# The first adaLN modulation as tiles of 128 channels, in a float32 trunk kernel

## The reference, cut to what matters

```python
h, hc = x, ctx                                   # 256 latent and 256 context tokens, D = 1024
silu_c, silu_cc = silu(c), silu(c_ctx)
for l in range(2):
    mod_lat = (silu_c @ ada_w[l] + ada_b[l]).reshape(b, 9, D)    # ada_w[l]: 1024 x 9216
    mod_ctx = (silu_cc @ ada_w[l] + ada_b[l]).reshape(1, 9, D)
    h = ffn_half(h, mod_lat, 0, ...)             # shift mod[0], scale mod[1], gate mod[2]
    hc = ffn_half(hc, mod_ctx, 0, ...)
    ...                                          # mixer with mod 3 to 5, second ffn_half with mod 6 to 8
return rmsnorm(h, final_norm_w)

def ffn_half(h, mod, k0, norm_w, wg, wu, wd):
    u = rmsnorm(h, norm_w) * (1 + mod[:, k0 + 1]) + mod[:, k0]
    return h + 0.5 * mod[:, k0 + 2] * ((silu(u @ wg) * (u @ wu)) @ wd)
```

## Time and profile before

| | |
|---|---|
| median of 3 runs | 1987.65 us (1984.37 to 1988.5) |
| the profiled execution, its own time | 1990.52 us |
| its span in the profile | 1988.9 us |
| mean granted TensorE clock | 0.992 |
| busy: TensorE, VectorE, ScalarE, GpSimd | 98%, 63%, 40%, 4% |

### The profile page before, as it was taken

How to read it: one execution, slowest core, us unless ns; L and a number is a source line. 1 busy time by engine, 2 the same in 40 slices (tenths; PEclk the granted TensorE clock), 3 DMA queues, 4 the chain that set the end, 5 groups by cost and what they waited for, 6 DMA issues and landing times.

```text
span 1988.9 us, 28983 instructions
## 1 busy us (share of the span) xinstructions
PE 1952.4 (98%) x10006; PEld 1654.5 (83%) x10006; DVE 1262.4 (63%) x2048; ACT 794.7 (40%) x1083; POOL 72.3 (4%) x142
## 2 busy tenths in 40 slices
PE   8999999999999999999999999999999998999998
PEld 3788888888888888888888888888888897899998
DVE  2657566676666466667576675756758687475555
ACT  2432222355654323532222354232225576456444
POOL 0000000000000000000000000000000000000000
PEclk8999999999999999999999999999999999999999
DMA  7246444433223243345445424544544333445564
GB/s 309 96 140 207 138 159 169 159 106 117 65 74 111 86 141 122 106 139 199 137 159 176 159 94 158 174 148 143 195 138 133 100 106 118 159 142 180 181 184 153
DMA packets 78664, 287.39 MB, mean 144 GB/s; under 512 B 8768, under 2 KB 10048, under 8 KB 77824
## 3 DMA queue, kind: packets, MB, share of 16 engines
q1 hardware_dynamic: 58912, 212.89, 32.4%
q0 software_dynamic: 19392, 73.34, 11.2%
q10 hardware_dynamic: 288, 0.18, 0.0%
HBM read 285.34 MB, written 1.05 MB: 144 GB/s over the span
## 4 chain that ended last, share of the span: by engine, by line
PE 93%; DMA 3%; DVE 2%; ACT 1%; issue 1%; SPq 0%; DVEq 0%; ACTq 0%
PE bank L332 26%; PE bank L334 26%; PE bank L333 26%; DMA raw<-weights 2%; PE bank L472 2%; PE bank L661 2%; PE bank L522 1%; PE bank L528 1%; PE bank L523 1%; PE bank L397 1%; PE bank L398 1%; PE bank L401 1%; ACT w_hi L684 1%; PE bank L360 1%; PE bank L605 1%
## 5 line engine op out<-in xcount | busy, mean ns | idle before, releaser
L332 PE MATMUL bank<-u_hi,w_hi 128*128 128x512 f32 (+1 forms) x1824 | 664.9, 365 | 3.5 <-DVE w_lo L950 3.4
L333 PE MATMUL bank<-u_lo,w_hi 128*128 128x512 f32 (+1 forms) x1824 | 655.2, 359 | 0.0
L334 PE MATMUL bank<-u_hi,w_lo 128*128 128x512 f32 (+1 forms) x1824 | 655.2, 359 | 0.0
L950 DVE TENSOR_TENSOR w_lo<-raw,w_hi 128x1024 fp32r<-128x1024 f32 x384 | 469.0, 1222 | 248.4 <-ACT w_hi L684 219.3
L684 ACT ACTIVATE w_hi<-raw 128x1024 fp32r<-128x1024 f32 x384 | 404.7, 1055 | 438.2 <-DMA raw<-weights 435.6
L332 PEld LDWEIGHTS bank<-u_hi,w_hi 128*128 128x128 f32 x1824 | 345.0, 189 | 55.6 <-DVE w_lo L950 4.9
L334 PEld LDWEIGHTS bank<-u_hi,w_lo 128*128 128x128 f32 x1824 | 344.7, 189 | 51.1
L333 PEld LDWEIGHTS bank<-u_lo,w_hi 128*128 128x128 f32 x1824 | 345.1, 189 | 50.6 <-issue 0.7
L332 PE MATMUL bank<-hid_hi,w_hi 128*128 128x512 f32 (+1 forms) x832 | 299.0, 359 | 1.4 <-DVE w_lo L950 1.1
L334 PE MATMUL bank<-hid_hi,w_lo 128*128 128x512 f32 (+1 forms) x832 | 298.3, 358 | 0.0
L333 PE MATMUL bank<-hid_lo,w_hi 128*128 128x512 f32 (+1 forms) x832 | 298.2, 358 | 0.0
(11 more groups left out here) (152 smaller groups left out, 1505.0 us busy)
## 6 DMA issues: line engine op xcount, KB each, us to landing
raw<-weights SPq DMA_DIRECT2D x384, 512.0 KB, 3.5
ada_raw<-adaw POOLq DMA_DIRECT2D x128, 512.0 KB, 4.2
start_w<-weights SPq DMA_DIRECT2D x8, 1024.0 KB, 12.3
box<-box POOLq DMA_DIRECT2D x4, 1024.0 KB, 8.2
h<-resid SPq DMA_DIRECT2D x1, 2048.0 KB, 19.4
silu_c<-c POOLq DMA_DIRECT2D x1, 1024.0 KB, 5.0
out<-sig_a SPq DMA_DIRECT2D x8, 128.0 KB, 2.0
poolw<-poolw POOLq DMA_DIRECT2D x2, 256.0 KB, 10.9
```

The lines of the kernel that those rows point to most:

```text
L332: pe.matmul(ps, w_hi[:, slot, k, :], hi(k), start=first, stop=False)
L333: pe.matmul(ps, w_hi[:, slot, k, :], lo(k), start=False, stop=False)
L334: mm = pe.matmul(ps, w_lo[:, slot, k, :], hi(k), start=False, stop=last)
L950: dve.tensor_tensor(view(w_lo, (j % RING) * UNIT, [1, UNIT]), raw[:, j % RING, :], view(w_hi, (j % RING) * UNIT, [1, UNIT]).bitcast(F32), ...
```

## The change

The 1024 x 2048 weights of the first shift and scale are stored as 11 column tiles and 5 row tiles of 512 KB. A column tile holds the weights of 128 output channels, with k on the partitions. It is the stationary operand, in 8 pieces of 128 x 128, and the two `silu(c)` columns move: the result is a pair of columns in a bank (`start_tile`). Scale and shift of chunks d = 0, 1, 2 (START_ROWS = 3) and the scale of d = 3 to 7 are made so; the shifts of d = 3 to 7 are made on VectorE from row tiles (`start_sum`), as the other modulation columns are.

TensorE makes the tiles of d = 0 and 1 first, those of d = 2 between the first norm's spread and the first chunk, and the one of d = k + 2 behind chunk k for k = 1 to 5. VectorE turns each into `scale_c` and `shift_c` of that chunk alone (`start_out`), and its order becomes, chunk by chunk: `start_sum`, `start_out`, `scaled`, `split_lo` (for d < 3), `low`. ScalarE's splits of the first three units and its silu of `silu_c` stand between the first chunks too. `h` is loaded in four pieces behind the first four tiles; `silu_c` moves from GpSimd's queue to SyncE's; GpSimd's other loads wait for the last `u_hi` of the first norm. The first 16 counts of `s_used` are given at the end of chunk 6. The first norm's totals go to banks 0 and 1. The copy of the masks moves behind the first part of the first FFN.

The diff, cut to its core:

```diff
+START_ROWS = 3
+START_BANK = (4, 6, 3, 4, 6, 3, 4, 6)
...
+        start_t = [sb(f"start_t{n}", [P, ND, P], F32, at_)[0] for n, at_ in enumerate(
+            [hid_hi_at + 4096 * n for n in range(8)] + [v_at, v_at + 4096, scan_at[0] + 8192])]
+        start_r, _ = sb("start_r", [P, ND - START_ROWS, D], F32, gs_at)
...
+        def total_bank(n, s):
+            return bank[s if n == 0 else 4 + 2 * s]
...
             sp.dma_start(c_cols[:], c_cols_in).then_inc(s_ccland, 16)
-            for k in range(ND):
-                sp.dma_start(start_w[k // 4][:, 2 * (k % 4):2 * (k % 4) + 2, :],
-                             weights[2 * k:2 * k + 2].rearrange("a p n -> p a n")).then_inc(s_start[k], 16)
-                if k == ND // 2 + 1:
-                    sp.dma_start(h[:], resid_in).then_inc(s_hland, 16)
-            for u in range(RING):
+            for k in range(2):
+                for j in range(2):
+                    sp.dma_start(start_t[2 * k + j][:], weights[2 * k + j]).then_inc(s_start[k], 16)
+            for k in range(ND // 2):
+                sp.dma_start(h[:, 2 * k:2 * k + 2, :], resid_in[:, 2 * k:2 * k + 2, :]).then_inc(s_hland[k], 16)
+            for j in range(2):
+                sp.dma_start(start_t[4 + j][:], weights[4 + j]).then_inc(s_start[2], 16)
+            for u in range(AHEAD):
                 sp.dma_start(raw[:, u, :], weights[START + u]).then_inc(s_raw[u], 16)
+            sp.dma_start(silu_c[:], c_in.partition_broadcast(P)).then_inc(s_cland, 16)
+            for d in range(START_ROWS, ND):
+                sp.dma_start(start_r[:, d - START_ROWS, :], weights[8 + d]).then_inc(s_srow[d - START_ROWS], 16)
+                sp.dma_start(start_t[3 + d][:], weights[3 + d]).then_inc(s_start[d], 16)
+                if d == START_ROWS + 1:
+                    sp.dma_start(raw[:, AHEAD, :], weights[START + AHEAD]).then_inc(s_raw[AHEAD], 16)
...
-            pool.wait_ge(s_diag, 1)
-            pool.dma_start(silu_c[:], c_in.partition_broadcast(P)).then_inc(s_cland, 16)
+            pool.wait_ge(s_uhi, ND)
...
-            def start_columns():
-
-                pe.wait_ge(s_load, 32)
-                for b in range(START):
-                    if b % 4 == 0:
-                        pe.wait_ge(s_rows, b // 4 + 1)
-                    mm = pe.matmul(bank[0][:, 2 * b:2 * b + 2], start_rows[0:2, b // 4, b % 4 * P:(b % 4 + 1) * P],
-                                   ident[0:2, 0:2], start=True, stop=True)
-                mm.then_inc(s_cols, 1)
+            def start_tile(n, ps):
+
+                for k in range(ND):
+                    mm = pe.matmul(ps, start_t[n][:, k, :], c_cols[:, k, :], start=(k == 0), stop=(k == ND - 1))
+                return mm
+
+            def start_columns(d):
+
+                ps = bank[START_BANK[d]]
+                if d >= START_ROWS:
+                    pe.wait_ge(s_colout, d - 2)
+                    pe.wait_ge(s_start[d], 16)
+                    start_tile(3 + d, ps[:, 0:2]).then_inc(s_cols, 1)
+                else:
+                    pe.wait_ge(s_start[d], 32)
+                    start_tile(2 * d, ps[:, 0:2])
+                    start_tile(2 * d + 1, ps[:, 2:4]).then_inc(s_cols, 1)
...
-                if n == 0:
-                    start_columns()
...
-                if n < 3 * NLAYER:
+                if n == 0:
+                    start_columns(2)
+                elif n < 3 * NLAYER:
...
+                    if n_norm == 0 and 1 <= k < ND - 2:
+                        start_columns(k + 2)
+                    if n_norm == 0 and k == ND - 2:
+                        mm.then_inc(s_used, START)
...
-            for u in range(START):
-                k, m = u // 2, u % 2
-                if m == 0:
-                    pe.wait_ge(s_start[k], 16)
-                for q in range(2):
-                    mm = pe.matmul(bank[2 * m + q][0:2, :], c_cols[:, k, :],
-                                   start_w[k // 4][:, u % ND, q * 512:(q + 1) * 512],
-                                   start=(k == 0), stop=(k == ND - 1))
-                mm.then_inc(s_used, 1)
+            start_columns(0)
+            start_columns(1)
             pe.wait_ge(s_const, 2)
+            pe.wait_ge(s_load, 32)
...
+                if i is not None or base + j - RING >= START:
...
-                    for j in range(AHEAD):
-                        split_next(START, None, j)
                 for d in range(ND):
+                    if n == 0 and d < AHEAD:
+                        split_next(START, None, d)
+                    if n == 0 and d == START_ROWS - 1:
+                        act.wait_ge(s_cland, 16)
+                        act.activation(silu_c[:], silu_c[:], ACT.Silu).then_inc(s_silu_c, 1)
...
+            def start_sum(d):
+
+                if d == START_ROWS:
+                    dve.wait_ge(s_silu_c, 3)
+                dve.wait_ge(s_srow[d - START_ROWS], 16)
+                for s in range(2):
+                    link(dve.scalar_tensor_tensor(
+                        out=junk[:, s, :], in0=start_r[:, d - START_ROWS, :], scalar=1.0, in1=silu_c[:, s, :],
+                        op0=ALU.mult, op1=ALU.mult, accum_out=mod[:, s, d:d + 1]))
+                link(dve.tensor_scalar(shift_c[:, :, d], mod[:, :, d], cols[:, C_ADAB + d:C_ADAB + d + 1], None, ALU.add))
+
+            def start_out(d):
+
+                ps = bank[START_BANK[d]]
+                dve.wait_ge(s_cols, d + 1)
+                if d < START_ROWS:
+                    link(dve.tensor_scalar(shift_c[:, :, d], ps[:, 2:4], cols[:, C_ADAB + d:C_ADAB + d + 1], None, ALU.add))
+                dve.scalar_tensor_tensor(out=scale_c[:, :, d], in0=ps[:, 0:2], scalar=cols[:, C_NORM + d:C_NORM + d + 1],
+                                         in1=view(mod, ND + d, [0, 2]), op0=ALU.mult, op1=ALU.add
+                                         ).then_inc(s_colout, 1)
+                dve.wait_ge(s_colout, d + 1)
...
-                    dve.wait_ge(s_cols, 1)
-                    link(dve.tensor_copy(mod[:, :, 0:START], view(bank[0], 0, [1, 2], [2, START])))
-                    norm_columns(0, 0, 0)
-                    for j in range(AHEAD):
-                        split_lo(START, None, j)
...
+                    if n == 0 and d >= START_ROWS:
+                        start_sum(d)
+                    if n == 0 and d > 1:
+                        start_out(d)
                     scaled(d)
-                    if d:
+                    if n == 0 and d < AHEAD:
+                        split_lo(START, None, d)
+                    if n == 0:
+                        low(d)
+                    elif d:
                         low(d - 1)
-                low(ND - 1)
+                if n:
+                    low(ND - 1)
...
-                    dve.wait_ge(s_silu_c, 3)
-                    dve.wait_ge(s_mland, 16)
-                    link(dve.tensor_copy(masks[:], masks_f[:]))
...
+            link(dve.scalar_tensor_tensor(out=mod[:, 0, ND:2 * ND], in0=cols[:, C_ADAB + ND:C_ADAB + 2 * ND], scalar=1.0,
+                                          in1=cols[:, C_NORM:C_NORM + ND], op0=ALU.add, op1=ALU.mult))
+            start_out(0)
             for d in range(ND):
                 add_squares(0, d)
-            for b in range(4):
-                dve.wait_ge(s_used, START - 1 + b // 2)
-                dve.tensor_copy(start_rows[0:2, b, :], bank[b][0:2, :]).then_inc(s_rows, 1)
+            start_out(1)
```

More of the change, by code:

```diff
@@ L145, in program @@
         v, v_at = sb("v", [P, 4, NH * P])
-        masks_f, _ = sb("masks_f", [P, NLEVEL, P], F32, v_at)
-        gs, _ = sb("gs", [P, 2, ALL])
+        masks_f, _ = sb("masks_f", [P, NLEVEL, P], F32, scan_at[0] + 12288)
+        gs, gs_at = sb("gs", [P, 2, ALL])
         sig_a, sig_a_at = sb("sig_a", [P, ND, ALL])
@@ L162, in program @@
         mix_t, _ = sb("mix_t", [P, 2, 2, ALL], F32, scan_at[1] + 4096)
-        start_w = [sb(f"start_w{n}", [P, START // 2, UNIT], F32, at_)[0] for n, at_ in enumerate((u_hi_at, hid_hi_at))]
-        start_rows, _ = sb("start_rows", [P, 4, 512], F32, scan_at[1] + 8192)
+        start_t = [sb(f"start_t{n}", [P, ND, P], F32, at_)[0] for n, at_ in enumerate(
+            [hid_hi_at + 4096 * n for n in range(8)] + [v_at, v_at + 4096, scan_at[0] + 8192])]
+        start_r, _ = sb("start_r", [P, ND - START_ROWS, D], F32, gs_at)
         head_t, _ = sb("head_t", [P, 2, ALL])
@@ L187, in program @@
         s_raw = [sem(f"raw_landed{i}") for i in range(RING)]
-        s_start = [sem(f"start_chunk_landed{k}") for k in range(ND)]
+        s_start = [sem(f"start_tiles_landed{k}") for k in range(ND)]
+        s_srow = [sem(f"start_rows_landed{k}") for k in range(ND - START_ROWS)]
         s_hi = sem("hi_ready")
@@ L194, in program @@
         s_load = sem("start_landed")
-        s_hland = sem("residual_landed")
+        s_hland = [sem(f"residual_landed{k}") for k in range(ND // 2)]
         s_mland = sem("masks_landed")
@@ L200, in program @@
```

(29 more changed lines are left out.)

2 lines of the change are left out of this document (removed).

## The result

The changed kernel takes 1991.15 us (1989.82 to 1992.47), the one before, timed beside it, 1985.35 us (1980.37 to 1990.98): a ratio of 1.0025, 95% interval [1.0014, 1.0037]. It is slower by some 5 us (2.8 to 7.3). The forecast of 1989.2 in 1984 to 1994 holds the time; the shift it forecast was +1.5. When both were timed again, later, the ratio was 1.0015 [1.0002, 1.0027].

A forecast was written before the change was run, and what follows sets the result against it. TensorE was taken as the bound, holding 93% of the span. The head's 14.7 us gain is given back to VectorE's steps (+0.3), the refill adds 1.2: +1.5 on the median 1987.65 gives 1989.2, range 1984 to 1994.

The forecast's parts named there:

- prediction's own measure of 4 us: Whole time: a measurement tells about 0.2% (4 us) from no change.
- Price of a narrow record: Tiles ahead of the chunks: 0.21 us a record at half clock, 0.11 at full; 0.21 taken for all.
- steps 1 to 3: Head up to the first chunk: tiles, totals, spread, d = 2 tiles; first chunk at 36.7 not 51.37, 14.7 us gained.
- cover of step 1: First four tiles, ending at 20.4: they hide the squares, delayed by `start_out(0)` to 19.7, by 0.7 us.
- Rival A: Tiles ahead of the chunks: narrow records warm the clock to 2.4 GHz; 11.5 us less, 1977.7; chance 0.10.
- Step 4: Chunks 0 and 1 run from half clock to full in 6.7 us, to 43.4; tile 3 at full clock, 1.8.
- Step 5: Chunks from d = 3: VectorE sets the pace, 5.3 us a step; chunk 7 ends 70.2 against 69.9, +0.3.
- Clock between the chunks: TensorE's 3.2 us stretches without wide work before chunks 6 and 7: a fall costs 0 to 1.8; taken as 0.
- rival B: Between the chunks: the clock drops, TensorE is the bound at 7.2 us a step; 2000; chance 0.09.
- Step 7: First refill: GpSimd's loads, moved behind `u_hi(7)`, share the DMA engines with it; +1.2 us, bounds 0 and 2.
- rival C: Chained products overlap and the refill isn't touched: 1986.8; chance 0.81 together with the forecast.

The follow-up runs named there:

- v1: Changed kernel with the wide dummies of e6, the three repairs of e7 and a 256-column dummy ahead of each later tile; ratio to before 1.0004.
- e2: Changed kernel with VectorE's two products of the next chunk's shift sum placed on either side of `low`; ratio to before 0.9995.
- e4: Changed kernel with three 512-column dummy matmuls between the tiles of d = 2 and chunk 0; ratio to before 1.0013.
- e9: Changed kernel with VectorE's five shift sums undone: all 16 tiles on TensorE, two behind each of chunks 1 to 5; ratio to before 1.0090.
- e3: Changed kernel with the shift sums of chunks 3 and 4 ahead of `start_out(3)`, later ones one chunk ahead; ratio to before 0.9997.
- e1: Changed kernel with GpSimd's first loads released by the third `u_hi` instead of the eighth; ratio to before 0.9994.
- e5: Kernel before, with GpSimd's first ada and masks loads waiting for the eighth `u_hi` and the masks' copy behind part 0; ratio to before 0.9998.
- e6: Changed kernel with 512-column dummies: three before the first tile, one behind each of six tiles, two in the diagonal wait; ratio to before 1.0041.
- before_again: Kernel before, unaltered, single run for a second trace; the unit behind the refill at 72.91 us, the mark at 412.24 us.
- e7: Changed kernel with GpSimd's loads released by the third `u_hi`, one sum more ahead of `start_out(3)`, sums on either side of `low`; ratio to before 0.9976.

## Why the prediction was right, and where its sum was off

The time lies in the range, and the mechanism was the one described: the head gains 14 us and gives them back. The size of the shift was not right: +1.5 was forecast, +5.0 measured (+3.0 the second time). The first of these is slower by the prediction's own measure of 4 us, and to slower it had given 0.17. That 1989.2 came within 2 us is in part luck: the three runs it started from had a median of 1987.65, the ten of the result 1985.35, from which +1.5 would have given 1986.9, over 4 us off. Point by point:

- **Price of a narrow record, steps 1 to 3: right.** 0.2155 and 0.207 measured for 0.21; 20.8 for 20.4, 34.5 for 34.1, chunk 0 at 37.31 for 36.7. Most of the last two differences is a slip of the sum: 25.8 and 2.1 make 27.9 for the end of the spread and not 27.4, and 27.88 was measured. The cover of step 1 held as well: the squares ended at 19.3, 1.4 us ahead of TensorE. Rival A is refuted: behind some 25 us of almost only narrow matmuls chunk 0 still started at half clock, 0.43 a wide record. The sign that the prediction named, a granted clock of 0.50, can't be read there, since PEclk shows 1.00. By the rule of the Trainium skill that the prediction set against its row ("TensorE: Matmul & The Clock Gate", Part 1: activity releases the throttle) the clock would have risen; this case disagrees for matmuls of one or two columns. v1 shows the same tiles at either price in one trace (2.06 and 3.20 us).
- **Step 4: right.** 6.4 us for 6.7, tile 3 in 1.69 for 1.8.
- **Step 5: right.** 5.3 us a round, shown to be the bound by e2 (TensorE waits in the chain and the round shortens when the wait for ScalarE is filled) and by e4 (TensorE waits in front of chunks 6 and 7, and the end is the same). In the changed kernel's second trace all rounds up to `u_hi(7)` are on the chain. `u_hi(7)` was done at 68.4 for 68.2, chunk 7 ended at 70.6 for 70.2.
- **Clock between the chunks: half right.** Taken as 0. In the changed kernel it fell at 58.8 and TensorE took the pace for chunks 5 and 6, as in rival B, but rose again in chunk 7 (69.1). Since VectorE's own round ended at the same place, this cost under 0.3 us. In the second trace it fell at 58.2, rose, and fell again at 68.4. Rival B's mechanism is real and e9 shows it in the open; at one tile a step it is hidden, but only just: in e3, with less on VectorE, it was the bound.
- **Step 7, the refill: right in kind, mis-sized.** +1.2 forecast with a bound of 2, 2.14 measured in the first trace and 1.3 in the second. e1, e3 and e5 show that the cost goes with how shortly before the refill GpSimd's loads are issued, as step 7 had it.
- **What no step had: the clock's fall behind the refill.** Behind the pause of 1.94 us in front of the unit the clock fell at 79.3, and some eight records took 0.43 or nearly: 1.6 us. The sum at the mark is 0.7 + 2.1 + 1.6 = 4.4, where the prediction had 0.3 + 1.2. In the second trace it didn't happen, and the mark is 1.9 earlier. That the pause causes the fall is not shown: e2 and e3 with pauses of 0.8 and 0.6 had none, e6 with one of 2.2 had one, but e4 with 2.34 had none.
- **The base of the sum: perhaps as large an error, not settled.** The sum was made against an execution 2.9 us above the median, and +1.5 was carried over to the median as if that surplus lay elsewhere. Some of it may lie in this very head: before_again and e5 put the mark 3.0 and 2.5 us earlier, since the clock fell later in the narrow records of line 351. Those records are gone in the change, with what chance there was in them. Against the mean of the three marks of before (413.4) the profiled execution was 1.8 late, and the two of the changed kernel (418.7) are 5.3 late, where the timed runs say 5.0 and 3.0. But three marks are few, and by the same mean e1 is 2.8 late at the mark and 1.2 ahead in time, and e7 is 1.7 ahead at the mark and 4.8 in time. So that mean may lie 2 to 3 us too low, which would leave nothing of this error, or the stretch behind the mark has a part in it.
- **The prediction's rival C** (nothing at the refill, a smaller step) fell: the round was the longest of its bounds.

What stays open: when a pause is followed by a fall (1.94 us in the changed kernel was, 2.34 in e4 wasn't), where the base of the sum lay, and why the kernel before spreads so much more than the changed one. None of it was tried.

## What to carry to other kernels

Work taken off the engine that is the bound pays only until another engine's round becomes the bound: count the round of the engine that gets the work, with its waits, before counting the gain. A load that is made to wait for "the last chunk done" starts right at the moment when the first refills start too; tie it to an earlier event when the DMA engines are idle. And before adding a sum to a median, look where in the profiled execution its distance to the median lies.

## What was not expected of the hardware

- Narrow matmuls aren't free: 128x128 float32 weights against 2 columns cost 0.21 us a record at half clock and 0.11 at full, and 13.8 us of them without a pause didn't raise the clock (chunk 0's wide records still took 0.43).
- One float32 matmul of 512 columns (1.92 us) behind each tile didn't raise it either over 22 us (0.50), while the same matmuls unbroken did within 5.3 us (e4).
- From the last wide matmul to the fall of the clock it was 2.3 us in one execution of the same kernel and 5.4 in another, which moved all behind it by about 3 us.
